# Attention on VectorE: weights, turned copies and scores of one step in another order, the reciprocals brought into the step of the scores

## What is computed

```
sc = einsum('bhcqd,bhckd->bhcqk', qi, k) * scale          # c: two score maps for one head
sc = where(key_pos <= q_pos, sc, NEG_INF)
p = softmax(sc, axis=-1)
a = p[:, :, 0] - lam * p[:, :, 1]
o = einsum('bhqk,bhkd->bhqd', a, v)                       # then an rms norm over each head
```

## Time and profile before

| | |
|---|---|
| median of three runs | 3853.85 us (3851.75 to 3857.58) |
| the profiled execution | 3861.44 us, its span in the profile 3859.6 us |
| mean granted clock of TensorE | 0.985 |
| busy, share of the span | PE 94%, DVE 30%, ACT 20%, POOL 11% |
| attention of the first block | from 662 us to about 1060 us |
| attention of the two layers | about 2330 to 2575 us, and 3115 to 3375 us |
| expert mixture | the stretch of about 1300 to 2280 us, in which the loads of expert weights run at 409 GB/s |

### The profile page before, as it was taken

One profiled execution on the slowest core, in us unless ns is written; L12 is line 12 of the kernel. 1 busy time (PEld: TensorE's weight loads), 2 busy tenths in 40 slices (PEclk: granted clock), 3 DMA queues, 4 the chain that ended last, 5 costly groups with the idle time before them and its releaser, 6 DMA issues.

```text
span 3859.6 us, 33017 instructions
## 1 busy us (share of the span) xinstructions
PE 3611.0 (94%) x12600; PEld 1742.4 (45%) x12600; DVE 1152.5 (30%) x2612; ACT 763.5 (20%) x1772; POOL 427.5 (11%) x393
## 2 busy tenths in 40 slices
PE   7999999999999888888887889999999999999999
PEld 3555555454444433323332344555444545554444
DVE  3356666243101303100111035443220144432211
ACT  2135554223102101000000022222110122221100
POOL 0003334021000000000000002101220021012200
PEclk9899999999999899999999999999999999999999
DMA  8423333112124699999999961012221211122120
GB/s 280 162 67 93 93 93 90 45 57 82 66 87 170 262 409 409 409 409 409 409 409 409 409 229 55 33 55 87 66 87 66 78 53 39 39 93 87 66 82 28
DMA packets 302209, 634.08 MB, mean 164 GB/s; under 512 B 32554, under 2 KB 145818, under 8 KB 301798
## 3 DMA queue, kind: packets, MB, share of 16 engines
q1 hardware_dynamic: 241278, 592.28, 41.0%
q10 hardware_dynamic: 60776, 39.70, 3.9%
HBM read 625.50 MB, written 10.24 MB: 165 GB/s over the span
## 4 chain that ended last, share of the span: by engine, by line
PE 73%; DMA 18%; DVE 4%; SPq 1%; ACT 1%; issue 1%; POOL 1%; DVEq 0%; POOLq 0%; ACTq 0%
PE psum L308 31%; PE psum L1642 9%; DMA arena<-in_w_exp_gate_dram 7%; DMA arena<-in_w_exp_up_dram 7%; PE psum L810 6%; PE psum L2445 4%; PE psum L2902 4%; PE psum L2938 4%; DMA arena<-in_w_exp_down_dram 4%; PE psum L1466 2%; PE psum L1494 2%; PE psum L1475 2%; PE psum L2923 1%; SPq L277 1%; PE psum L2371 1%
## 5 line engine op out<-in xcount | busy, mean ns | idle before, releaser
L308 PE MATMUL psum<-arena 128*128 128x512 f32 (+1 forms) x3200 | 1301.3, 565 | 2.6 <-POOL arena L2044 2.4
L308 PEld LDWEIGHTS psum<-arena 128*128 128x128 f32 x3200 | 608.1, 192 | 675.4 <-issue 653.4
L2445 PE MATMUL psum<-arena 128*64 128x512 f32 x3072 | 692.9, 596 | 143.9 <-DMA arena<-in_w_exp_up_dram 74.4
L2445 PEld LDWEIGHTS psum<-arena 128*64 128x64 f32 x3072 | 232.8, 136 | 585.2 <-issue 566.7
L1642 PE MATMUL psum<-arena 128*128 128x512 f32 x768 | 344.3, 602 | 0.0
L810 PE MATMUL psum<-arena 128*128 128x512 f32 (+1 forms) x768 | 256.2, 491 | 1.1 <-DVE arena L550 1.1
L1642 PEld LDWEIGHTS psum<-arena 128*128 128x128 f32 x768 | 144.3, 191 | 187.1 <-issue 186.2
L2981 POOL TENSOR_SCALAR arena<-arena 128x512 f32<-128x512 f32 x88 | 138.3, 1572 | 687.4 <-ACT arena L2960 687.4
L1574 DVE CUSTOM_DVE_ANT_0 arena<-psum,arena 128x512 f32<-128x512 f32 (+3 forms) x224 | 113.7, 545 | 302.2 <-PE psum L1466 302.2
L2987 DVE SCALAR_TENSOR_TENSOR arena<-arena 128x512 f32<-128x512 f32 x88 | 66.3, 753 | 426.4 <-POOL arena L2981 426.4
L810 PEld LDWEIGHTS psum<-arena 128*128 128x128 f32 x768 | 144.6, 191 | 107.9 <-issue 96.3
(11 more groups left out here) (276 smaller groups left out, 2885.2 us busy)
## 6 DMA issues: line engine op xcount, KB each, us to landing
arena<-in_w_exp_gate_dram SPq DMA_DIRECT2D x128, 1024.0 KB, 18.6
arena<-in_w_exp_up_dram SPq DMA_DIRECT2D x128, 1024.0 KB, 18.5
arena<-in_w_exp_down_dram SPq DMA_DIRECT2D x128, 1024.0 KB, 18.7
arena<-in_w_in_dram SPq DMA_DIRECT2D x64, 1024.0 KB, 5.2
arena<-in_w_up_dram SPq DMA_DIRECT2D x88, 512.0 KB, 4.8
arena<-in_w_ada_dram SPq DMA_DIRECT2D x24, 1024.0 KB, 9.1
arena<-in_w_down_dram SPq DMA_DIRECT2D x20, 1024.0 KB, 5.1
arena<-acs_scratch ACTq DMA_DIRECT2D x64, 256.0 KB, 6.0
```

What stands on the lines that cost most here:

```text
L308: mm = pe.matmul(shaped(b, l, r), l, r, start=kt == 0, stop=kt == nkt - 1)
L2445: mm = pe.matmul(banks[n][64 * j:64 * j + 64, :], lhs[:, kt, 64 * j:64 * j + 64], w, start=kt == 0, stop=kt == 2 * nkb - 1)
```

## The change

It reorders the parts of one step of DVE's attention. The reciprocals and the product with lambda of a unit move from the start of the next step to the place right behind its scores, and the copy of the turned bank goes from behind the scores to ahead of them. No instruction is added, removed or resized, and no other engine's list changes.

```diff
-            yield from att2_steps(J, (1, sums), (1, weights), (0, scores), (2, turned), (3, outs), (4, heads))
+            yield from att2_steps(J, (1, weights), (2, turned), (0, scores), (0, sums), (3, outs), (4, heads))
```

## The result

| | before | after |
|---|---|---|
| median of the runs compared (four each) | 3854.05 us (3851.75 to 3857.58) | 3834.3 us (3832.14 to 3835.91) |
| the profiled execution | 3861.44 us | 3834.35 us, its span 3832.5 us |
| mean granted clock | 0.985 | 0.984 |

The ratio is 0.9942, with a 95% interval of 0.993 to 0.9955: 0.58% faster, 19.75 us between the medians. The forecast was 3842.4 us, a gain of 0.30%, with a range from 3833.

A forecast was written before the change was run, and what follows sets the result against it. TensorE, busy 94%, was taken as the bound, with 30.9 us of its waits on VectorE at stake. First block 4.7 plus 3.4 for each layer made 11.5 us, so 3842.4 us from 3853.85; range 3833 to 3856.

The forecast's parts named there:

- the eight short waits: Scores in the layers waiting for a bank: all go, four a layer, 1.1 us, of which 0.8 counted.
- the clock: TensorE's drops to 1.2 GHz after idle or short matmuls, about 1.3 us each: 4 us either side, no sign.
- first pair: Layer steps `[0, 1] * 4`, waits of 1.25 and 1.21 us: VectorE becomes the chain, only 0.6 us won.
- The step of 2.00 us: First block, step behind an output copy: scores start at 827.5 instead of 828.0, winning 0.5 us of the 2.00.
- GpSimd's early start: `two` units: L1661 stands until GpSimd is done, 0.2 us lost a layer; other bound 0.7 us won.
- The heads: Layers, wait for weights with five head instructions between, 3.2 us once a layer: 0, between -0.3 and +0.3 us.
- second pairs: Layers, second pair of transpose waits in `[0, 1] * 4`: VectorE's idle time takes up the stand, 2.46 us won.
- behind heads: One step a layer with heads, rope and V copy in a row: 0.3 us lost, between -0.8 and +0.5.
- first block: `NEAR` attention: three waits of 1.41 us go, 4.2 us, and 0.5 us of a fourth; 4.7 us won.
- Rival B: More than summed: clock holds in three or four more places, GpSimd doesn't block; 18 us, 3836 us; chance 0.12.
- Rival C: Attention: TensorE waits for late weights (L1586 or L1581) instead of L1595; 3850 us, inside 0.2%; chance 0.24.
- Rival D: `two` units of the layers: VectorE's stand for exponentials delays the weights; 8 us slower, 3862 us; chance 0.12.

## Why the prediction fell short

**Right: the place and the kind.** The long waits for L1595 went because VectorE was idle ahead of the scores; the new waits came where they were named. VectorE's idle time ahead of L1561, foretold as about 100 us of new one, is 86.8 us, of which 19.3 were there before (source view of the reciprocals, idle before them):

```profile
  ACT arena L1514: 86.8, 224
```

**Wrong: the term of the eight short waits.** This is the step of the sum that failed. "So they go: four in each layer, 1.1 us", of which 0.8 counted, took the recorded idle time as the price. The three counted in each layer are worth 3.5 us, both layers together 7.0 instead of 1.6. The wait put in by hand and the copy for `two` units only show it apart from everything else: a wait between the two score matmuls of a unit costs its idle time and one whole matmul. Counting only recorded waits also missed the late second map in the heads. The row with `x2` on either side of the wait and 0.91 us for each half was there to be read before, beside an `x4` of 0.91.

**Outside the sum: the clock.** The prediction had it at 4 us to either side with no sign. Behind the short waits three low-clock stretches went, 5.0 us; in exchange one came behind the first pair of each layer. Timeline, PE, the place of the earlier trace rows in the changed kernel, then with the copy alone:

```profile
2498.49 0.30 PE L1475 MATMUL psum<-arena 128*128 128x128 f32 x1 [1.39 <-DVE arena L1586]
2499.19 0.33 PE L1475 MATMUL psum<-arena 128*128 128x128 f32 x1 [0.40 <-DVE arena L1595]
2499.45 3.58 PE L1494 MATMUL psum<-arena 128*64 128x512 f32 x16
```

```profile
2482.57 0.30 PE L1475 MATMUL psum<-arena 128*128 128x128 f32 x1 [0.69 <-DVE arena L1586]
2483.27 0.33 PE L1475 MATMUL psum<-arena 128*128 128x128 f32 x1 [0.40 <-DVE arena L1595]
2483.53 2.38 PE L1494 MATMUL psum<-arena 128*64 128x512 f32 x16
```

**The first pair.** The chain of VectorE was worked out rightly: idle time 1.39 + 0.40 = 1.79 us instead of 2.46, a gain of 0.67 where 0.6 was said. But behind the longer single gap the same sixteen matmuls took 3.58 us instead of 2.38, and the scores after them 1.35 instead of 0.92. Up to these sixteen the place had gained 0.8 us; the low clock took 1.6, and so it lost 0.8 us. The granted clock of 2494 to 2506 is 0.86; with the copy alone neither the gap of 1.39 nor the low clock is there. Why the chip lowers the clock at the one and not at the other isn't settled.

**The step of 2.00 us.** The stand of the output copy was foreseen, and its size was right: the scores start at 823.47, and as this trace is 3.92 us ahead when it enters attention, that is 827.39 in the times of the kernel before; 827.5 was said, and 827.98 is what the kernel before has. PE waits 2.29 us there because it is through its transposes that much earlier. The gain of 0.6 us became a loss of 0.4 by the clock: before, the low stretch (825.93 to 829.35) lay on the transposes and the scores, which took 1.97 and 1.79 us instead of 1.09 and 1.13; now it lies on dense filler (824.52 to 827.93). The scores before:

```profile
827.98 1.79 PE L1466 MATMUL psum<-arena 64*128 64x512 f32 x4
```

**GpSimd's early start.** I took the end of the range in which L1661 is held, from the earlier trace rows. It isn't held: 0.69 us in all six places of the changed kernel where it ran beside L1631 for more than 0.01 us, and 1.06 to 1.10 in the nine where GpSimd had started L1653 before it. The row that I used had the other kind of GpSimd instruction. The larger mean of L1661 that was foretold did not come (806 ns before, 808 after). At the transposes behind the weights the chain had gained 0.8 us in either layer, so it was the other bound, 0.7 us, that held. Low-clock stretches then took part of it back, and 0.46 us in layer 0 and 0.08 in layer 1 were left. The total of L1581 hides this: the wait became 4.60 instead of 2.56 us because PE comes earlier to it, and it swallows what the short wait and a low-clock stretch ahead of it had given (3.1 us, of which 2.6 were lost again).

**The heads.** They were put at 0 and gave 0.1 and 1.15 us. In each layer 0.6 us are the late second map told above, and 0.3 us the wait for the weights, which fell from 3.24 to 2.95 us. The rest, a loss of 0.8 us in layer 0 and a gain of 0.2 in layer 1, is where low-clock stretches fall; why they fall there stays open.

Sum of the differences to the prediction: short waits 5.4, clock behind them 5.0, heads 1.3, 512-key units 0.9, second pairs 0.8, behind heads 0.2, first pairs -2.8, first block -0.2: 10.6 us, and 21.95 - 11.5 = 10.45 is what was found, the same within the rounding. So the two terms that made the forecast too small are the short waits, priced by their idle time alone, and the low-clock stretches behind them, for which the sum had nothing. Rival B had the right size (18 us) for partly the right reasons: the clock and the free GpSimd were in it, the paired matmuls in none. Rival C happened in the first pair, where it was expected, and by 0.35 us in the step behind the heads. Rival D fell: the weights of the `two` units did not come later. The stand that it fears does cost when the copy is behind it, 47 us, but by late banks and not by late weights (L1581 fell to 4.6 us there).

## What to carry to other kernels

Where matmuls on different rows of the array run as a pair, a wait between the two costs a whole matmul beside its idle time: look for a group that is recorded as `x2` and `x2` with the full duration each, or that is longer than its sisters at the same clock, and price it from there. Put the copy that frees a bank ahead of work that waits anyway, and an instruction that stands for another engine's result behind all that others wait for. Take a change of order apart: here one half gave about 28 us in attention and the other took some 7 back.

## What the runs showed of the hardware

The second of two score matmuls is free while they run as a pair: 0.91 us for both with 384 keys, 1.13 with 512, and 1.24 us more for a unit of 512 keys once they are separated.

A VectorE product with two SBUF inputs that starts beside a running GpSimd `TENSOR_TENSOR` ends about 0.55 us behind it (1.06 to 1.10 us, 0.99 with a repeated second input), and one beside a GpSimd `TENSOR_SCALAR` isn't held (0.69 us). The Trainium skill, page "SBUF — State Buffer", section "Summary: rules for kernel authors", has such an instruction blocked beside any GpSimd instruction that reads SBUF. For `TENSOR_TENSOR` the trace agrees; for `TENSOR_SCALAR`, which reads SBUF too, page and measurement differ, and the measurement decides: here it was not held. Whether the number of inputs is the reason or something else in which the two instructions differ, no run separates.

On GpSimd, a product of 128x512 with one factor a partition took 1.57 us as `TENSOR_SCALAR` and 1.04 us as `TENSOR_TENSOR` with the factor repeated.
